# The convolution branch of the gated mixers of a four-layer fp32 model: from behind the attention's projection into the head steps

## The chip, the cores and the metric

One core of a Trainium2 chip runs the whole program in one launch. The metric is the device time of one execution in microseconds (us), lower is better. Everything is fp32; TensorE multiplies in a mode that keeps fewer bits, so each operand is split in a high and a low part.

## What is computed

256 tokens of width 1024 go through two blocks of two layers each. The first block's layer is a gated mixer (heads with a decaying state, and a short convolution) and then a feed-forward network: dense in layer 0, eight experts in layer 1. The second block's layers are of another kind and untouched here. The part that matters, from the reference:

```python
q, f_logit, i_in, g_out, b_gate, c_gate, u, gate_a, gate_b = split_projection(h, w_in)
...
o = hgrn2_chunk_recurrence(qh, k, heads(i_in), log_f)
o = rms_norm(o, g_norm_w) * jax.nn.silu(heads(g_out))
y_a = jnp.einsum('bse,ed->bsd', o.reshape(bsz, seq, HGRN_VAL_WIDTH).astype(h.dtype), w_proj_hgrn)
v = b_gate * u
vp = jnp.pad(v, ((0, 0), (CONV_K - 1, 0), (0, 0)))
conv = conv_w[0] * vp[:, 0:seq, :]
for j in range(1, CONV_K):
    conv = conv + conv_w[j] * vp[:, j:j + seq, :]
y_b = jnp.einsum('bse,ed->bsd', c_gate * conv, w_proj_conv)
merged = jax.nn.sigmoid(gate_a) * y_a + jax.nn.sigmoid(gate_b) * y_b
return jnp.einsum('bsd,de->bse', merged, w_out)
```

## The kernel before, in words

**The stream of weights.** All weights lie in one array of slabs, 128 partitions by 2048 numbers (1 MB), in the order of use. SyncE loads them six ahead into `raw` (`Sync.slabs`). For each, ScalarE copies the high part to `whi` (`hi`, L305, two halves), VectorE subtracts to get the low part in `wlo` (`lo`, L746), and TensorE runs 24 matmuls (`slab`, L1333 to L1335: high by high, low by high, high by low). `whi` holds three slabs: `hi` of slab n waits until slab n-3 is done on TensorE. Each engine runs its instructions in the order written, so the place of a `hi()` or `lo()` among the other calls decides when a slab is ready.

**The mixer** (`mixer1`, for l = 0 and 1). Twelve slabs give the first three of nine column segments. Then four **head steps** (`it` = 0 to 3), two heads each: TensorE turns their inputs (`head_turn`), sums the logs of the decay (`head_sums`), multiplies scores (`head_scores`, L1445) and outputs (`head_out`, L1464). Between these stand six slabs a step (`late_half`): each pair gives 512 columns of a late segment, which `late_group` on ScalarE (L359, L360) copies out. PSUM banks 0 to 3 serve these pairs in turn, banks 4 to 7 the heads. VectorE multiplies the decays (`decay`, L842) and picks the scores (`select`, L855).

**The tail**, twelve slabs, is written out on every engine:
1. ScalarE ends the norm and takes Silu of g_out and Sigmoid of both gates (L447 to L451); VectorE multiplies the heads' output with norm and gate (L891, event `on`) and b_gate with u (L894, `bu`). TensorE waits for `on`, turns the product (L1365) and, once it is split (L317, L763), projects it: a.mm0 and a.mm1, two slabs each.
2. TensorE turns `bu` and c_gate (L1502, four pairs of columns, c0 to c6, 32 transposes) into banks 4 to 7. For each pair VectorE takes the three taps and the product with c_gate straight from PSUM (L910, L914, L917). ScalarE (L460) and VectorE (L921) split the result into XH and XL; then b.mm0 and b.mm1, four slabs.
3. VectorE gates and adds both (L903, L925, L926), TensorE turns the sum (L1365), and w2.mm0, w2.mm1 (four slabs) give the output, which is added to X (L932).

## Time and profile before

| | us |
|---|---|
| median of three runs | 3032.9 (3029.36 to 3033.09) |
| the profiled execution, its own time | 3030.92 |
| its span in the profile | 3029.1 |
| TensorE busy in it | 2849.8 |
| VectorE busy | 2054.6 |
| ScalarE busy | 1686.7 |
| mean granted TensorE clock | 0.973 |

A busy TensorE is not always TensorE at full speed: the granted clock stands beside it in the views by stretch (1.00 is 2.4 GHz, 0.50 is 1.2 GHz). Idle time in brackets is time of that engine just before the instruction, with the instruction that ended it.

### The profile page before, as it was taken

What the parts mean: (1) busy time and instruction counts of PE and PEld (TensorE: products, weight loads), DVE (VectorE), ACT (ScalarE), POOL (GpSimd) and SP (SyncE); (2) the same over time, 40 slices, a digit from 0 to 9 for tenths busy, and PEclk for the clock granted to TensorE, in tenths of its full rate; (3) what the DMA queues carried; (4) which work ended last, traced back from release to release, by engine and by line L of the source; (5) the groups of instructions that cost most, each with busy time, mean ns of one, the idle gap of its engine ahead of it and who ended that gap; (6) DMA issues with size and microseconds to landing.
All of it is one profiled execution on the core that took longest, in us unless ns stands there. A gap on an engine that the chain in (4) does not pass through costs nothing.

```text
span 3029.1 us, 34232 instructions
## 1 busy us (share of the span) xinstructions
PE 2849.8 (94%) x13288; PEld 2355.1 (78%) x13288; DVE 2054.6 (68%) x2910; ACT 1686.7 (56%) x2271; POOL 33.0 (1%) x55
## 2 busy tenths in 40 slices
...
GB/s 230 154 135 111 131 176 185 170 173 139 131 108 163 376 357 347 342 355 357 352 344 352 359 193 183 185 158 148 142 171 184 177 183 192 148 157 147 160 185 107
DMA packets 173657, 633.63 MB, mean 209 GB/s; under 512 B 19520, under 2 KB 19520, under 8 KB 173488
## 3 DMA queue, kind: packets, MB, share of 16 engines
...
## 4 chain that ended last, share of the span: by engine, by line
PE 86%; DVE 9%; ACT 3%; issue 1%; DMA 1%; SPq 0%; DVEq 0%; ACTq 0%; POOLq 0%
PE ps L1333 26%; PE ps L1335 26%; PE ps L1334 26%; DVE wlo L746 2%; PE ps L1445 2%; DVE CA L1207 2%; PE ps L1522 1%; PE ps L1569 1%; PE ps L1365 1%; PE ps L1431 0%; PE ps L1432 0%; DVE XN L914 0%; DVE Z L1294 0%; DMA raw<-in_W 0%; ACT whi L305 0%
## 5 line engine op out<-in xcount | busy, mean ns | idle before, releaser
L746 DVE TENSOR_TENSOR wlo<-raw,whi 128x1024 fp32r<-128x1024 f32 x1182 | 1386.6, 1221 | 539.6 <-ACT whi L305 533.0
L305 ACT ACTIVATE whi<-raw 128x1024 fp32r<-128x1024 f32 x1182 | 1187.7, 1057 | 558.2 <-PE ps L1335 552.3
L1333 PE MATMUL ps<-whi,XH 128*128 128x512 f32 (+1 forms) x2192 | 871.1, 397 | 43.5 <-DVE XL L764 19.8
L1334 PE MATMUL ps<-wlo,XH 128*128 128x512 f32 (+1 forms) x2192 | 857.3, 391 | 0.0
L1335 PE MATMUL ps<-whi,XL 128*128 128x512 f32 (+1 forms) x2192 | 856.6, 391 | 0.0
L1333 PEld LDWEIGHTS ps<-whi,XH 128*128 128x128 f32 x2192 | 416.4, 190 | 137.1 <-DVE XL L764 23.6
L1335 PEld LDWEIGHTS ps<-whi,XL 128*128 128x128 f32 x2192 | 415.8, 190 | 87.9
L1334 PEld LDWEIGHTS ps<-wlo,XH 128*128 128x128 f32 x2192 | 416.5, 190 | 82.4 <-issue 0.5
L1333 PE MATMUL ps<-whi,XEH 128*128 128x512 f32 x704 | 280.8, 399 | 1.4 <-DVE XEL L995 1.4
L1335 PE MATMUL ps<-whi,XEL 128*128 128x512 f32 x704 | 275.3, 391 | 0.0
L1334 PE MATMUL ps<-wlo,XEH 128*128 128x512 f32 x704 | 274.1, 389 | 0.0
L1333 PE MATMUL ps<-whi,GH 128*128 128x512 f32 x440 | 172.2, 391 | 0.0
L1335 PE MATMUL ps<-whi,GL 128*128 128x512 f32 x440 | 171.3, 389 | 0.0
L1334 PE MATMUL ps<-wlo,GH 128*128 128x512 f32 x440 | 171.2, 389 | 0.0
L1335 PEld LDWEIGHTS ps<-whi,XEL 128*128 128x128 f32 x704 | 132.1, 188 | 28.9
L1333 PEld LDWEIGHTS ps<-whi,XEH 128*128 128x128 f32 x704 | 132.2, 188 | 27.7 <-DVE XEL L995 1.6
L1334 PEld LDWEIGHTS ps<-wlo,XEH 128*128 128x128 f32 x704 | 132.5, 188 | 25.9
L484 ACT ACTIVATE GH<-ps 128x512 fp32r<-128x512 f32 x55 | 33.0, 599 | 206.9 <-PE ps L1522 206.9
L952 DVE TENSOR_TENSOR GL<-ps,GH 128x512 fp32r<-128x512 f32 x55 | 38.0, 692 | 162.3 <-ACT GH L484 162.3
L1333 PE MATMUL ps<-whi,GH_ 128*128 128x512 f32 x352 | 144.2, 410 | 0.0
L1335 PE MATMUL ps<-whi,GL_ 128*128 128x512 f32 x352 | 137.4, 390 | 0.0
L1334 PE MATMUL ps<-wlo,GH_ 128*128 128x512 f32 x352 | 137.3, 390 | 0.0
...
## 6 DMA issues: line engine op xcount, KB each, us to landing
...
```

Of the source, the lines that this page charges most:

```text
L305: act.activation(k.whi[:, slot, part], k.raw[:, at, part], ACT.Copy).then_inc(*k.up("act_hi"))
L484: act.activation(GH[:, 2 * g:2 * g + 2, :], src, ACT.Copy).then_inc(*k.up("act_split", f"{T}.gh{g}"))
L746: dve.tensor_tensor(k.wlo[:, at, part], k.raw[:, at, part], k.whi[:, slot, part], ALU.subtract).then_inc(*k.up("dve_lo"))
L952: dve.tensor_tensor(GL[:, 2 * g:2 * g + 2, :], src, GH[:, 2 * g:2 * g + 2, :], ALU.subtract).then_inc(*k.up("dve_split", f"{T}.gl{g}"))
L1207: x = dve.scalar_tensor_tensor(out=CA[:, c, :], in0=HP[:, c, j:j + S], scalar=dw(c, j), in1=CA[:, c, :], op0=ALU.mult, op1=ALU.add)
L1333: pe.matmul(ps, xh, k.whi[:, slot, cols], start=first, stop=False)
L1334: pe.matmul(ps, xh, k.wlo[:, at, cols], start=False, stop=False)
L1335: mm = pe.matmul(ps, xl, k.whi[:, slot, cols], start=False, stop=last)
L1365: mm = pe.transpose(bank[:, i * S + t * P:i * S + (t + 1) * P], src(2 * b + i, t), k.ident[:])
L1445: mm = pe.matmul(o, x, x, start=True, stop=True)
L1522: mm = pe.transpose(turned[:, fb, t * P:(t + 1) * P], GN[:, t, fb * P:(fb + 1) * P], k.ident[:])
L1569: mm = pe.matmul(k.ps[:, 6 + c // 4, (c % 4) * P:(c % 4 + 1) * P], k.XN[:, t, c * P:(c + 1) * P], k.PM[:, t, :], start=t == 0, stop=t == N ...
```

## The change

1. The late segments come in another order (`LATE`, and with it the weights' order in `stream`): the convolution's b, u, c columns first (head steps 0 and 1), then g_out, gate_a, gate_b. The scratch segment `SKN` moves to gate_b's place.
2. In head steps 1 and 2 TensorE turns one pair of columns after `head_sums` and one after the second `head_scores` (`conv_turn`, eight transposes each, 32 in all) into the banks of the late pairs; ScalarE copies them to SBUF (`conv_turned`), into the parts of q and f that are used up.
3. In head steps 1 to 3 VectorE multiplies b by u in two halves (`conv_gate`) and takes the taps, now from SBUF (`conv3`); ScalarE and VectorE split the result into new arrays CVH and CVL (`conv_split`, `conv_rest`). The last half of the last split (`conv_rest(1)`) stands behind the head steps.
4. The tail begins with b.mm0 and the first slab of b.mm1; then TensorE turns the heads' output (now into banks 4 to 7), does the second slab of b.mm1, then a.mm0 and a.mm1. The turning of the merged sum is cut in two (`ya` between the slabs of a.mm1, `yb` after the first slab of w_out), and w_out's slabs come in the order 0, 2, 1, 3. `hi` and `lo`, twelve each as before, are spread singly among this work.

`turned` and `project` get arguments for other targets and for a call between two slabs, nothing else. No instruction is left out; the mixers of both layers change alike. The diff, cut:

```diff
-SKN = SCU
+SKN = SGB
+LATE = [(SCB, 0), (SCU, 0), (SCC, 0), (SCB, 1), (SCU, 1), (SCC, 1), (SGO, 0), (SGO, 1), (SGA, 0), (SGA, 1), (SGB, 0), (SGB, 1)]
+CONV_FREES = {5: 0, 6: 1, 8: 2, 9: 3}
...
+            ("pad3", [P, SCC * SEG], F32), ("CVH", [P, KT, S], F32R), ("CVL", [P, KT, S], F32R),
...
+    def conv_out(self):
+        return self.Z[:, SCU * SEG:(SCU + 1) * SEG].rearrange("p (n c) -> p n c", c=S)
+    def conv_in(self, n):
+        at = (SQ if n % 2 == 0 else SF) * SEG
+        return self.Z[:, at:at + 2 * CW].rearrange("p (i c) -> p i c", i=2)
...
     def late_group(self, T, it, j):
         act, k = self.eng, self.k
-        bank = 2 * ((3 * it + j) % 2)
-        src, at = k.ps[:, bank:bank + NT, :], it * (NT * CW) + (SGA, SGO, SCB)[j] * SEG
-        to = k.Z[:, at:at + NT * CW].rearrange("p (t c) -> p t c", t=NT)
+        n = 3 * it + j
+        bank = 2 * (n % 2)
+        src, to = k.ps[:, bank:bank + NT, :], k.seg(LATE[n][0])[:, LATE[n][1]]
         act.wait_ge(*k.at(f"{T}u{j}.mm.{it}"))
         act.activation(to[:, 0], src[:, 0], ACT.Copy, scale=k.rsin[:, 0:1])
...
+    def conv_turned(self, T, n, bank):
+        act, k = self.eng, self.k
+        act.wait_ge(*k.at(f"{T}c{n}.tp"))
+        if n >= 2:
+            act.wait_ge(*k.at(f"{T}c{n - 2}.y"))
+        act.activation(k.conv_in(n), k.ps[:, bank:bank + 2, :], ACT.Copy).then_inc(*k.up("act_evac", f"{T}c{n}.in"))
+    def conv_split(self, T, g):
+        act, k = self.eng, self.k
+        act.wait_ge(*k.at(f"{T}c{2 * g + 1}.y"))
+        act.activation(k.CVH[:, 4 * g:4 * g + 4, :], k.conv_out()[:, 4 * g:4 * g + 4, :], ACT.Copy).then_inc(*k.up("act_split", f"{T}cv{g}.h"))
...
+            if it == 1 or it == 2:
+                self.conv_turned(T, 2 * it - 2, 2 * (it % 2))
             self.late_group(T, it, 1)
             self.hi()
+            if it >= 2:
+                self.conv_split(T, it - 2)
             self.hi()
+            if it == 1 or it == 2:
+                self.conv_turned(T, 2 * it - 1, 2 * ((it + 1) % 2))
             self.head_cross(T, it)
             self.late_group(T, it, 2)
+            if it == HEADS // 2 - 1:
+                self.hi()
             self.head_out(T, it)
         act.wait_ge(*k.at(f"{T}o1.{HEADS // 2 - 1}"))
         act.activation(k.orn, k.oss, ACT.Sqrt, scale=1.0 / P, bias=k.eps).then_inc(*k.up("act_step", T + "orms"))
-        act.wait_ge(*k.at(f"{T}ev2.{HEADS // 2 - 1}"))
+        act.wait_ge(*k.at(T + "ev1.2"))
         act.activation(k.seg(SGO), k.seg(SGO), ACT.Silu).then_inc(*k.up("act_step", T + "g"))
-        act.activation(k.seg(SGA), k.seg(SGA), ACT.Sigmoid)
-        act.activation(k.seg(SGB), k.seg(SGB), ACT.Sigmoid).then_inc(*k.up("act_step", T + "gates"))
+        self.hi()
+        act.wait_ge(*k.at(T + "ev2.3"))
+        act.activation(k.seg(SGB), k.seg(SGB), ACT.Sigmoid).then_inc(*k.up("act_step", T + "gb"))
+        self.hi()
...
+        self.turned(T + "o", lambda i: gw, bank0=4)
+        self.hi()
+        act.wait_ge(*k.at(T + "ev0.3"))
+        act.activation(k.seg(SGA), k.seg(SGA), ACT.Sigmoid).then_inc(*k.up("act_step", T + "ga"))
+        self.hi(2)
+        self.turned(T + "ya", None, KT // 2, 0, 4, k.CVH)
+        self.hi(2)
+        self.turned(T + "yb", None, KT // 2, KT // 2, 6, k.CVH)
         self.hi(4)
...
+    def conv_gate(self, T, g):
+        dve, k = self.eng, self.k
+        dve.wait_ge(*k.at(f"{T}ev1.{g}"))
+        B = k.seg(SCB)[:, g]
+        dve.tensor_tensor(B, B, k.seg(SCU)[:, g], ALU.mult).then_inc(*k.up("dve_gate", f"{T}bu{g}"))
+    def conv3(self, T, l, n):
+        dve, k = self.eng, self.k
+        CV = k.conv_out()
+        w = lambda j, i: k.pcols[:, l * LCOLS + 17 + 8 * j + i:l * LCOLS + 18 + 8 * j + i]
+        dve.wait_ge(*k.at(f"{T}c{n}.in"))
+        dve.wait_ge(*k.at(f"{T}bu{n // 2}"))
+        pair = [(2 * n + i, k.conv_in(n)[:, i, :]) for i in range(2)]
+        for i, src in pair:
+            c = dve.tensor_scalar(CV[:, i, :], src[:, 0:S], w(2, i), None, ALU.mult)
+        self.step(c)
+        for j in (1, 2):
+            for i, src in pair:
+                c = dve.scalar_tensor_tensor(out=CV[:, i, j:], in0=src[:, 0:S - j], scalar=w(2 - j, i), in1=CV[:, i, j:], op0=ALU.mult, op1=ALU.add)
+            self.step(c)
+        dve.tensor_tensor(CV[:, 2 * n:2 * n + 2, :], CV[:, 2 * n:2 * n + 2, :], k.conv_in(n)[:, :, S:], ALU.mult).then_inc(*k.up("dve_gate", f"{T}c{n}.y"))
+    def conv_rest(self, T, g):
+        dve, k = self.eng, self.k
+        at = slice(4 * g, 4 * g + 4)
+        dve.wait_ge(*k.at(f"{T}cv{g}.h"))
+        dve.tensor_tensor(k.CVL[:, at, :], k.conv_out()[:, at, :], k.CVH[:, at, :], ALU.subtract).then_inc(*k.up("dve_split", f"{T}cv{2 * g + 1}.l"))
...
+            if it == 1 or it == 2:
+                self.conv_gate(T, it - 1)
+            if it >= 2:
+                self.conv3(T, l, 2 * it - 4)
+            if it == 3:
+                self.conv_rest(T, 0)
...
+            if it >= 2:
+                self.conv3(T, l, 2 * it - 3)
...
+        self.lo()
+        self.conv_rest(T, 1)
...
+        self.lo()
+        YA, YB = k.seg(SQ), k.seg(SF)
+        dve.wait_ge(*k.at(T + "gb"))
+        dve.wait_ge(*k.at(T + "b.mm0"))
+        dve.tensor_tensor(YB[:, 0], ps[:, 0:2, :], k.seg(SGB)[:, 0], ALU.mult).then_inc(*k.up("dve_step", T + "b.ev0"))
+        self.lo()
         gw = pc[:, c0 + 16:c0 + 17]
-        self.turned(T + "o", lambda i: gw)
-        YA, YB = k.seg(SQ), k.seg(SF)
+        self.turned(T + "o", lambda i: gw, bank0=4)
+        self.lo()
+        dve.wait_ge(*k.at(T + "b.mm1"))
+        dve.tensor_tensor(YB[:, 1], ps[:, 2:4, :], k.seg(SGB)[:, 1], ALU.mult).then_inc(*k.up("dve_step", T + "b.ev1"))
+        self.lo()
+        dve.wait_ge(*k.at(T + "ga"))
         for j in range(2):
-            self.lo(2)
             dve.wait_ge(*k.at(f"{T}a.mm{j}"))
+            self.step(dve.tensor_tensor(YA[:, j], ps[:, 2 * j:2 * j + 2, :], k.seg(SGA)[:, j], ALU.mult), f"{T}a.ev{j}")
+            dve.tensor_tensor(YA[:, j], YA[:, j], YB[:, j], ALU.add).then_inc(*k.up("dve_gate", f"{T}merged{j}"))
+            self.lo()
             if j == 0:
...
+                self.turned(T + "ya", None, KT // 2, 0, 4, (k.CVH, k.CVL))
+                self.lo()
+        self.turned(T + "yb", None, KT // 2, KT // 2, 6, (k.CVH, k.CVL))
+        self.lo(2)
...
+            self.lo()
             dve.wait_ge(*k.at(f"{T}w2.mm{j}"))
...
+                if n in CONV_FREES:
+                    pe.wait_ge(*k.at(f"{T}c{CONV_FREES[n]}.in"))
...
+    def conv_turn(self, T, n, it, j):
+        pe, k = self.eng, self.k
+        g, bank = n // 2, 2 * ((3 * it + j) % 2)
+        pe.wait_ge(*k.at(f"{T}bu{g}"))
+        pe.wait_ge(*k.at(f"{T}ev2.{g}"))
+        pe.wait_ge(*k.at(f"{T}ev{j}.{it}"))
+        for i in range(2):
+            for a, s in enumerate((SCB, SCC)):
+                for t in range(NT):
+                    c = (2 * n + i) % 4
+                    mm = pe.transpose(k.ps[:, bank + i, a * S + t * P:a * S + (t + 1) * P], k.seg(s)[:, g, t, c * P:(c + 1) * P], k.ident[:])
+        mm.then_inc(*k.up("pe_turn", f"{T}c{n}.tp"))
...
+            if it == 1 or it == 2:
+                self.conv_turn(T, 2 * it - 2, it, 0)
             self.late_half(T, it, 1, 1)
...
+            if it == 1 or it == 2:
+                self.conv_turn(T, 2 * it - 1, it, 1)
             self.late_half(T, it, 2, 1)
...
+        y = lambda half: lambda i, t: YA[:, half, t, i * P:(i + 1) * P]
+        pe.wait_ge(*k.at(T + "ev1.3"))
+        self.project(T + "b.mm0", 0, split=T + "cv", XH=k.CVH, XL=k.CVL)
+        pe.wait_ge(*k.at(T + "ev2.3"))
+        self.project(T + "b.mm1", 2, XH=k.CVH, XL=k.CVL, split=T + "cv", between=lambda: self.turned(
+            T + "o", [T + "on0"], lambda i, t: O[:, i // 4, t, (i % 4) * P:(i % 4 + 1) * P], bank0=4, ready2=[T + "on1"]))
+        pe.wait_ge(*k.at(T + "b.ev0"))
+        self.project(T + "a.mm0", 0, split=T + "o")
+        pe.wait_ge(*k.at(T + "b.ev1"))
+        self.project(T + "a.mm1", 2, split=T + "o", between=lambda: self.turned(T + "ya", [T + "merged0"], y(0), KT // 2, 4))
+        pe.wait_ge(*k.at(T + "ya1.l"))
+        self.slab(self.columns(0, 0, k.CVH, k.CVL))
+        self.turned(T + "yb", [T + "merged1"], y(1), KT // 2, 6)
+        self.slab(self.columns(0, 2, k.CVH, k.CVL))
+        pe.wait_ge(*k.at(T + "yb1.l"))
+        self.slab(self.columns(1, 0, k.CVH, k.CVL), T + "w2.mm0")
+        self.slab(self.columns(1, 2, k.CVH, k.CVL), T + "w2.mm1")
...
+        late = [q[{SGO: 3, SCB: 4, SCC: 5, SCU: 6, SGA: 7, SGB: 8}[s]][l][:, g * CW:(g + 1) * CW] for s, g in LATE]
+        parts.append(column_slabs(np.concatenate([q[n][l] for n in (1, 0, 2)] + late, 1)))
+        parts += [column_slabs(i[n][l]) for n in ("w_proj_conv", "w_proj_hgrn")]
+        parts.append(column_slabs(i["w_out"][l])[[0, 2, 1, 3]])
```

How that moves instructions, at three places. **VectorE, from the last select of head step 2 into head step 3** (L890 was L855, L780 was L746, L853 was L818). Before:

```order
L855 COPY_PREDICATED SM<-masks,ps 128x256 x7
L746 TENSOR_TENSOR wlo<-raw,whi 128x1024 x4
L818 TENSOR_TENSOR LFL<-Z,LFH 128x256 x2
L746 TENSOR_TENSOR wlo<-raw,whi 128x1024 x2
L842 TENSOR_TENSOR XN<-XN,KQ 128x64 x4
```

and changed:

```order
L890 COPY_PREDICATED SM<-masks,ps 128x256 x7
L780 TENSOR_TENSOR wlo<-raw,whi 128x1024 x2
L909 TENSOR_SCALAR Z<-Z,pcols 128x256 x2
L913 SCALAR_TENSOR_TENSOR Z<-Z,pcols 128x255 x2
L913 SCALAR_TENSOR_TENSOR Z<-Z,pcols 128x254 x2
L915 TENSOR_TENSOR Z<-Z 128x512
L922 TENSOR_TENSOR CVL<-Z,CVH 128x1024
L780 TENSOR_TENSOR wlo<-raw,whi 128x1024 x2
L853 TENSOR_TENSOR LFL<-Z,LFH 128x256 x2
L780 TENSOR_TENSOR wlo<-raw,whi 128x1024 x2
```

One pair's taps and half of the low parts now stand ahead of the step's first `lo`; another pair's taps (the same four rows) stand ahead of the decays.

**ScalarE, from the last head's output to the tail's first slabs** (the slab's split, L305, is now L317; L317 before and L329 now split the turned heads' output). Before:

```order
L409 ACTIVATE Z<-ps 128x2x128
L413 ACTIVATE SC,small<-ps 128x128 x2
L447 ACT_TABLE_LOAD
L447 ACTIVATE small<-small 128x16
L449 ACT_TABLE_LOAD
L449 ACTIVATE Z<-Z 128x2048
L450 ACT_TABLE_LOAD
L450 ACTIVATE Z<-Z 128x2048
L451 ACTIVATE Z<-Z 128x2048
L317 ACTIVATE XH<-ps,pcols 128x256
```

and changed:

```order
L421 ACTIVATE Z<-ps 128x2x128
L425 ACTIVATE SC,small<-ps 128x128 x2
L481 ACT_TABLE_LOAD
L481 ACTIVATE small<-small 128x16
L483 ACT_TABLE_LOAD
L483 ACTIVATE Z<-Z 128x2048
L317 ACTIVATE whi<-raw 128x1024 x2
L486 ACT_TABLE_LOAD
L486 ACTIVATE Z<-Z 128x2048
L317 ACTIVATE whi<-raw 128x1024 x2
L329 ACTIVATE XH<-ps,pcols 128x256
```

A slab's high part now stands behind Silu, another behind the one Sigmoid that is left here; a third stands ahead of the last two heads' output (L421, twice).

**VectorE, from the last select to the first gate of the tail.** Before:

```order
L855 COPY_PREDICATED SM<-masks,ps 128x256 x7
L746 TENSOR_TENSOR wlo<-raw,whi 128x1024 x2
L888 RECIPROCAL small<-small 128x16
L891 SCALAR_TENSOR_TENSOR Z<-Z,small 128x128 x16
L894 TENSOR_TENSOR Z<-Z 128x2048
L763 SCALAR_TENSOR_TENSOR XL<-ps,pcols,XH 128x256
```

and changed:

```order
L890 COPY_PREDICATED SM<-masks,ps 128x256 x7
L780 TENSOR_TENSOR wlo<-raw,whi 128x1024 x4
L922 TENSOR_TENSOR CVL<-Z,CVH 128x1024
L965 RECIPROCAL small<-small 128x16
L968 SCALAR_TENSOR_TENSOR Z<-Z,small 128x128 x16
L780 TENSOR_TENSOR wlo<-raw,whi 128x1024 x2
L975 TENSOR_TENSOR Z<-ps,Z 128x1024
L780 TENSOR_TENSOR wlo<-raw,whi 128x1024 x2
L798 SCALAR_TENSOR_TENSOR XL<-ps,pcols,XH 128x256
```

The last low parts of the convolution now wait behind one more `lo`, and the split of the heads' output (L798) behind two `lo` and a gate.

## Rows read from the trace of the kernel before

**Rows 1.** The page's part 4, the chain that ended last, share of the span by engine
```profile
PE 86%; DVE 9%; ACT 3%; issue 1%; DMA 1%; SPq 0%; DVEq 0%; ACTq 0%; POOLq 0%
```

**Rows 2.** Stretches of one core: busy us (instructions) by engine, granted clock, DMA
```profile
228.00:275.00 47.00, 47.00 (x257) 40.55 (x256) 30.56 (x87) 25.30 (x49) 0.00 (x0) 1.00 0.41 135
...
275.90:381.40 105.50, 81.50 (x352) 66.53 (x352) 64.34 (x97) 43.31 (x58) 0.00 (x0) 0.85 0.35 119
...
832.00:937.60 105.60, 81.74 (x353) 66.68 (x352) 64.35 (x97) 43.33 (x58) 2.27 (x5) 0.85 0.38 127
```

**Rows 3.** TensorE by line, 275.9 to 381.4 us: count, busy, mean ns, idle before
```profile
L1333 PE MATMUL ps<-whi,XH 128*128 128x512 f32 x96 | 39.5, 411 | 8.3 <-issue 6.1 <-DVE XL L764 2.1
...
L1502 PE MATMUL ps<-ident,Z 128*128 128x128 f32 x32 | 5.8, 349 | 4.4 <-DVE XN L917 4.4
...
L1365 PE MATMUL ps<-ident,Z 128*128 128x128 f32 x32 | 5.7, 337 | 11.3 <-DVE Z L891 9.5 <-DVE Z L926 1.7
```

**Rows 4.** TensorE in time: start, us, what, count, idle before it and releaser
```profile
275.27 0.61 PE L1464 MATMUL ps<-Z,SC 128*128 128x128 f32 x4
...
285.35 3.73 PE L1365 MATMUL ps<-ident,Z 128*128 128x128 f32 x16 [9.47 <-DVE Z L891]
...
291.22 0.50 PE L1333 MATMUL ps<-whi,XH 128*128 128x512 f32 x1 [2.14 <-DVE XL L764]
...
331.00 0.77 PE L1333 MATMUL ps<-whi,XH 128*128 128x512 f32 x1 [6.06 <-issue]
...
382.69 1.97 PE L1365 MATMUL ps<-ident,X 128*128 128x128 f32 x16 [1.32 <-DVE X L932]
```

**Rows 5.** ScalarE in time, splits of slabs in the tail
```profile
298.60 2.01 ACT L305 ACTIVATE whi<-raw 128x1024 fp32r<-128x1024 f32 x2 [5.76 <-PE ps L1335]
...
304.04 2.01 ACT L305 ACTIVATE whi<-raw 128x1024 fp32r<-128x1024 f32 x2 [3.43 <-PE ps L1335]
...
339.26 2.01 ACT L305 ACTIVATE whi<-raw 128x1024 fp32r<-128x1024 f32 x2 [7.01 <-PE ps L1335]
```

**Rows 6.** TensorE in time, turning the heads' inputs in head step 3
```profile
234.92 0.60 PE L1414 MATMUL ps<-ident,XN 128*128 128x128 f32 x4
...
235.71 0.48 PE L1333 MATMUL ps<-whi,XH 128*128 128x512 f32 x1
```

**Rows 7.** VectorE in time, head step 3 and tail of the first mixer
```profile
234.73 2.36 DVE L746 TENSOR_TENSOR wlo<-raw,whi 128x1024 fp32r<-128x1024 f32 x2 [6.13 <-ACT whi L305]
...
245.42 3.34 DVE L842 TENSOR_TENSOR XN<-XN,KQ 128x64 f32<-128x64 f32 x24 [5.39 <-ACT XN L391]
...
272.49 2.36 DVE L746 TENSOR_TENSOR wlo<-raw,whi 128x1024 fp32r<-128x1024 f32 x2
...
283.11 4.29 DVE L891 SCALAR_TENSOR_TENSOR Z<-Z,small 128x128 f32<-128x128 f32 x16 [3.04 <-ACT Z L449]
...
316.06 0.87 DVE L910 TENSOR_SCALAR XN<-ps,pcols 128x256 f32<-128x256 f32 x2
...
319.45 0.87 DVE L910 TENSOR_SCALAR XN<-ps,pcols 128x256 f32<-128x256 f32 x2
...
381.41 1.23 DVE L932 TENSOR_TENSOR X<-ps,X 128x1024 f32<-128x1024 f32 x1 [1.99 <-PE ps L1335]
```

**Rows 8.** ScalarE in time, head step 3 and what follows it
```profile
241.46 0.69 ACT L359 ACTIVATE Z<-ps,small 128x512 f32<-128x512 f32 x1 [2.92 <-PE ps L1335]
...
265.10 2.00 ACT L305 ACTIVATE whi<-raw 128x1024 fp32r<-128x1024 f32 x2 [5.87 <-PE ps L1335]
...
275.32 0.69 ACT L360 ACTIVATE Z<-ps,small 128x512 f32<-128x512 f32 x1
...
278.18 1.28 ACT L447 ACT_TABLE_LOAD   x1
...
279.48 0.31 ACT L447 ACTIVATE small<-small 128x16 f32<-128x16 f32 x1
...
281.10 1.91 ACT L449 ACTIVATE Z<-Z 128x2048 f32<-128x2048 f32 x1
```

More of the change, by code:

```diff
@@ L306, in hi, with turned @@
             self.n += 1
-    def turned(self, tag, gain, n=KT, at=0, bank0=0):
+    def turned(self, tag, gain, n=KT, at=0, bank0=0, into=None):
         act, k = self.eng, self.k
@@ L752, in step, with turned @@
         self.eng.wait_ge(*self.k.now("dve_step"))
-    def turned(self, tag, gain, n=KT, at=0, bank0=0):
+    def turned(self, tag, gain, n=KT, at=0, bank0=0, into=None):
         dve, k = self.eng, self.k
+        XH, XL = into or (k.XH, k.XL)
         for b in range(n // 2):
@@ L901, in mixer1 @@
             if j == 0:
-                dve.wait_ge(*k.at(T + "gates"))
-            dve.tensor_tensor(YA[:, j], ps[:, 2 * j:2 * j + 2, :], k.seg(SGA)[:, j], ALU.mult).then_inc(*k.up("dve_step", f"{T}a.ev{j}"))
-        CV = flat(k.XN[:]).rearrange("p (n c) -> p n c", c=S)
-        w = lambda j, i: pc[:, c0 + 17 + 8 * j + i:c0 + 18 + 8 * j + i]
-        for n in range(0, KT, 2):
-            pair = [(i, ps[:, 4 + i % 4, :]) for i in (n, n + 1)]
-            dve.wait_ge(*k.at(f"{T}c{n}.tp"))
-            for i, bank in pair:
-                c = dve.tensor_scalar(CV[:, i, :], bank[:, 0:S], w(2, i), None, ALU.mult)
-            self.step(c)
-            for j in (1, 2):
-                for i, bank in pair:
-                    c = dve.scalar_tensor_tensor(out=CV[:, i, j:], in0=bank[:, 0:S - j], scalar=w(2 - j, i), in1=CV[:, i, j:], op0=ALU.mult, op1=ALU.add)
-                self.step(c)
-            for i, bank in pair:
-                c = dve.tensor_tensor(CV[:, i, :], CV[:, i, :], bank[:, S:], ALU.mult)
-            c.then_inc(*k.up("dve_gate", f"{T}c{n}.y"))
@@ L919, in mixer1 @@
-        for i in range(0, KT, 2):
-            dve.wait_ge(*k.at(f"{T}cv{i}"))
-            dve.tensor_tensor(k.XL[:, i:i + 2, :], CV[:, i:i + 2, :], k.XH[:, i:i + 2, :], ALU.subtract).then_inc(*k.up("dve_split", f"{T}cv{i // 2}.l"))
-        for j in range(2):
-            self.lo(2)
-            dve.wait_ge(*k.at(f"{T}b.mm{j}"))
-            self.step(dve.tensor_tensor(YB[:, j], ps[:, 2 * j:2 * j + 2, :], k.seg(SGB)[:, j], ALU.mult), f"{T}b.ev{j}")
-            dve.tensor_tensor(YA[:, j], YA[:, j], YB[:, j], ALU.add).then_inc(*k.up("dve_gate", f"{T}merged{j}"))
```

47 lines of the change are left out of this document (9 added, 38 removed).

## The prediction

> **What bounds the kernel now.** I read the chain of waits first: TensorE carries 86% of the span, VectorE 9% [rows 1]. So only time in which TensorE stands, or runs at the lower clock, can be had without removing work. The view by stretches shows where that is. In a head step TensorE is busy all the time (47.00 of 47.00 us, clock 1.00) while VectorE works 30.6 and ScalarE 25.3. In the two tails it is busy 81.5 of 105.5 and 81.7 of 105.6 us, at a mean clock of 0.85 [rows 2]. TensorE's groups by line name the idle time of the first tail: 8.3 + 4.4 + 11.3 = 24.0 us [rows 3], nearly all in three holes: 9.5 us until the heads' output is normed and gated, 2.1 until it is split, and 6.1 + 4.4 round the convolution's taps [rows 3, 4].
>
> The holes cost a second time, in clock. 16 transposes take 3.73 us behind the first hole and 1.97 at the full clock [rows 4]. Slabs in a row end every 5.44 us (298.60 to 304.04), while the slab begun at 291.22 is done at 298.60 (7.4 us) and the one begun at 331.00 at 339.26 (8.3 us) [rows 4, 5]. That is 1.8 + 1.9 + 2.8 = 6.5 us, and the last 16 of the convolution's transposes, also at half clock, add some 2: 32 of them took 5.8 us of busy time [rows 3]. Together about 8.6 us of clock.
>
> **What the tail needs without holes.** The first tail runs from 275.88 (275.27 + 0.61) to 381.41, when VectorE has the last product: 105.5 us [rows 4, 7]. Its twelve slabs need 12 x 5.44 = 65.3 us, and after the change 16 + 8 + 8 transposes at 1.97 us per 16 = 3.9 us, together 69.2. The convolution's 32 transposes move into the head steps. There eight of them cost 0.79 us from first to next slab (234.92 to 235.71) and some 0.1 of slower restart [rows 6], so 4 x 0.9 = 3.6 us, in a stage where TensorE has no idle time: all of it is paid. Gain per mixer: 105.5 - 69.2 - 3.6 = 32.7 us, which agrees with idle plus clock (24.0 + 8.6 = 32.6). It holds only if each event is early enough. I walk the queues on the clock of the old trace; the 3.6 us shift all engines alike.
>
> **Head steps.** VectorE gets one pair's taps (316.06 to 319.45: 3.4 us) and, at one edge, a half product or half split (1.2 us, as the same size at 381.41) ahead of the step's first `lo`, and 3.4 us ahead of the decays. The waits there are 6.1 and 5.4 us [rows 7], against 4.6 and 3.4: both fit, with 1.5 and 2.0 us left, and 30.6 + 8.0 = 38.6 us of work stays under the step's 47. The trace has the taps only from PSUM. From SBUF I bound them at 2.5 us a pair (three of seven instructions at half price) and 5 (half as long again); at 5 the first wait is overrun by 0.1 and the second not at all. I take 3.4. ScalarE's copy of 1024 columns takes about 1.0 us (two such take 2.00) and it waits 5.9 us in one place of the step [rows 8]; one copy or split at each of three places fits. The evacuation for which the first `conv_turn` of a step waits is made from 241.5 to 242.7, while TensorE has two sums and a whole slab (5.4 us) to do behind the pair's end at 241.2: `conv_turn` can't come before 246.6, so it finds the bank free, 4 us early or more [rows 5, 6, 8]. The second has a slab and the scores before it. If this cover were gone, TensorE would pay the overrun one for one.
>
> **Tail, first event.** Nothing is between the last head and b.mm0's first slab: its weights are ready (`lo` done at 274.85) [rows 7] and half the convolution is split. First slab 275.6 to 281.2. The second needs `conv_rest(1)`, behind a `lo`, behind the new `hi`. ScalarE is free at 275.9 (275.32 + 0.6), `hi` ends at 277.9, `lo` at 279.3, `conv_rest` at 280.5. That is 0.7 us early, the thinnest margin.
>
> **Heads' output.** The new `hi` delays ScalarE by 1.9 us. From table load to Silu's end was 278.18 to 283.0, now to 285.0; the 16 products take 4.3 us [rows 7, 8] and end at 289.4. TensorE has three slabs to run, until 292.1: 2.7 early, so the 9.5 us hole is covered. Its split (0.39 us each, eight, behind two `lo` and one gate) has its first half at 296.9, needed at 299.6.
>
> **Later seams.** Counting 5.44 a slab, 2.0 a `lo` on ScalarE, 2.35 on VectorE, 1.23 a gate or sum: `lo` for the second slab of a.mm1 ends at 315.3 (needed 316.9), the first merged half at 313.0 (315.9), the `lo` of w_out's first slab at 320.8 (322.3), of its second at 327.1 (328.7), of its third at 332.6 (334.2). Each has 1.5 us or more. A stalled `hi` on ScalarE would hold the turned copies behind it; the late one is then `ya`, 4 us ahead of need. The last product ends near 345.2.
>
> The loads move by nothing but their pace: SyncE still waits for the slab six back, and the head stretch moves 135 GB/s, the tail 119 [rows 2]. In the second tail POOL's loads now meet the same slabs. I cost it at 0, at worst 1 us.
>
> **Sum.** Two mixers at 32.7 = 65.4 us; I take off 1.5 for semaphores on thin margins: 64 us. 3030.9 (the profiled execution, 2 below the median of 3032.9) less 64 is **2967 us**. Its own bounds: 2963 (all of it, and a fast draw like the lowest run) to 2973 (3 us lost per mixer).
>
> **A rule against the change.** A table load takes 1.28 us, and the next ScalarE instruction starts 1.30 us after it (278.18 to 279.48) [rows 8]. The Trainium skill, ScalarE: Activation LUTs, section "What ACT_TABLE_LOAD costs", adds a drain of some 1.38 us to each switch of set. By that rule, with Sqrt, Silu and Sigmoid now standing before slabs' splits, the heads' split would be some 4 us later and the sum by its figure about 3 us smaller, 2970. The trace does not show such a drain.
>
> **Rivals.**
> - *The tail keeps small waits* (0.14). For it: 0.7 and 1.5 us are thin, and `lo`, gate and split now alternate in one queue. Against: no length is guessed, all are read. If the second slab and four later seams each come 1.5 to 2.5 us late past need, a mixer loses 4 to 9 us: 2975 to 2985. The table loads are one way to it: if each cost twice its 1.28 us, the two ahead of the products would put the `lo` behind these at 294.3 (needed 294.0), the three ahead of the split would put its first half at 300.7 (needed 299.6): 1.4 us a mixer, 2970.
> - *Head steps 2 and 3 stretch* (0.06). VectorE's longer queue delays `lo` and decays; 2 us in each of four steps give 8 us: 2975. Against: the waits above.
> - *The clock does not come back* (0.05). If the lower clock had another cause than the idle time before it, 2 x 8.6 = 17 us stay: 2984. Against: it falls only behind the holes, and head steps run dense at 1.00 [rows 2].
> - *The change is hidden* (0.02). If the head steps were held as long as the tail gains, within 6 us: 3025 to 3037. I know no cause.
> - *Slower* (0.03). `conv_turn` waits on TensorE for `ev` and `bu`, ahead of a slab; ScalarE's next `hi` waits for that slab, and VectorE's taps for the copy. If this ring closed late in each of the 8 places (4 per mixer), every stall would also bring half clock for a slab (2.8 us). It decides at 65 / 8 = 8.2 us each, a stall of 5.4; at 7 us of stall the kernel takes 2967 + 8 x 9.8 = 3045. Against: `ev` is 4 us early or more, and `bu` needs no more than a gap of VectorE.
>
> The likeliest case has 0.70. The range 2961 to 2979 holds it, with the nearer part of the first two rivals, and leaves out under 2 in 10. Faster by over 0.2% (6 us, about what a measurement can tell here): 0.70 + 0.14 + 0.06 + 0.05 = 0.95; same 0.02; slower 0.03.
>
> **What would show it.** In the changed profile: two tails of 69 to 73 us with clock 0.98 or more; no idle of TensorE over 2 us in them; head steps 1 and 2 longer by 1.8 us each, step 3 not; idle of VectorE in steps 2 and 3 down by 8 and 9 us. The forecast is wrong if TensorE waits for CVL at the tail's second slab by more than 1 us, for XL at a.mm0, or for `lo` at w_out's slabs, or if a wait for the copy of a turned pair shows in a head step.

## The result, and the profile after

The changed kernel takes 2965.8 us (median of four, 2964.75 to 2966.68) against 3033.0 of the kernel before in the same session (3029.36 to 3034.6): 0.978 of its time, 95% interval 0.9763 to 0.9797. The forecast was 2967 in 2961 to 2979. The span fell from 3029.1 to 2962.9 us, by 66.2.

The chain that ended last, share of the span by engine (against [rows 1]):

```profile
PE 88%; DVE 8%; ACT 2%; issue 1%; DMA 1%; SPq 0%; DVEq 0%; ACTq 0%; POOLq 0%
```

By stretch, columns as in [rows 2] (busy us of TensorE, its weight loads, VectorE, ScalarE and GpSimd, then TensorE's granted clock and the DMA's share and rate): head step 2 and head step 3, each from the last output matmuls of one step to those of the next, then the two tails:

```profile
185.57:233.62 48.05, 48.05 (x266) 41.53 (x265) 37.04 (x104) 27.56 (x50) 0.00 (x0) 1.00 0.39 132
233.62:279.89 46.27, 46.27 (x251) 39.82 (x250) 35.83 (x98) 25.62 (x48) 0.00 (x0) 1.00 0.41 137
280.50:349.40 68.90, 68.84 (x320) 57.07 (x319) 47.41 (x62) 40.35 (x54) 0.00 (x0) 1.00 0.54 181
803.00:872.50 69.50, 69.44 (x326) 57.67 (x324) 47.41 (x62) 40.95 (x55) 2.27 (x5) 1.00 0.57 194
```

The tails of [rows 2] had 105.5 us, 81.5 of them busy, at a clock of 0.85. Now TensorE is never without work in them and stays at 1.00. Its groups by line in the first tail (against [rows 3]) have no idle time before any of them; the two other groups from CVH and CVL have 24.9 us each, the three from XH 12.5 us for 32 each. The 32 transposes, heads' output and merged sum, take 4.0 us where they took 5.7:

```profile
L1399 PE MATMUL ps<-whi,CVH 128*128 128x512 f32 x64 | 25.2, 393 | 0.0
...
L1431 PE MATMUL ps<-ident,Z 128*128 128x128 f32 x32 | 4.0, 272 | 0.0
```

TensorE in time, start and length in us, at the tail's two ends (against [rows 4]): the last head, the first slab 0.36 us behind it, the turning of half the merged sum between two slabs, and the only two waits, both behind the mixer:

```profile
279.89 0.61 PE L1549 MATMUL ps<-Z,SC 128*128 128x128 f32 x4
280.25 0.48 PE L1399 MATMUL ps<-whi,CVH 128*128 128x512 f32 x1
...
320.20 1.03 PE L1431 MATMUL ps<-ident,Z 128*128 128x128 f32 x8
320.99 0.48 PE L1399 MATMUL ps<-whi,XH 128*128 128x512 f32 x1
...
350.66 1.97 PE L1431 MATMUL ps<-ident,X 128*128 128x128 f32 x16 [1.32 <-DVE X L998]
353.95 0.50 PE L1399 MATMUL ps<-whi,XH 128*128 128x512 f32 x1 [1.32 <-DVE XL L799]
```

VectorE in time: a pair's taps, the split, the next waits (against [rows 7]), then what the heads' output needs and the two ends of the merged sum:

```profile
232.26 0.61 DVE L909 TENSOR_SCALAR Z<-Z,pcols 128x256 f32<-128x256 f32 x2
232.91 1.79 DVE L913 SCALAR_TENSOR_TENSOR Z<-Z,pcols 128x255 f32<-128x255 f32 x4
234.73 0.69 DVE L915 TENSOR_TENSOR Z<-Z 128x512 f32<-128x512 f32 x1
235.34 1.22 DVE L922 TENSOR_TENSOR CVL<-Z,CVH 128x1024 fp32r<-128x1024 f32 x1
239.34 2.36 DVE L780 TENSOR_TENSOR wlo<-raw,whi 128x1024 fp32r<-128x1024 f32 x2 [2.78 <-ACT whi L317]
...
250.03 3.35 DVE L877 TENSOR_TENSOR XN<-XN,KQ 128x64 f32<-128x64 f32 x24 [2.31 <-ACT XN L403]
...
283.89 1.22 DVE L922 TENSOR_TENSOR CVL<-Z,CVH 128x1024 fp32r<-128x1024 f32 x1
...
289.62 4.29 DVE L968 SCALAR_TENSOR_TENSOR Z<-Z,small 128x128 f32<-128x128 f32 x16 [3.04 <-ACT Z L483]
...
316.28 1.22 DVE L987 TENSOR_TENSOR Z<-Z 128x1024 f32<-128x1024 f32 x1
...
349.38 1.23 DVE L998 TENSOR_TENSOR X<-ps,X 128x1024 f32<-128x1024 f32 x1 [1.95 <-PE ps L1401]
```

ScalarE in time, the table loads (against [rows 8]):

```profile
284.69 1.28 ACT L481 ACT_TABLE_LOAD   x1
285.99 0.31 ACT L481 ACTIVATE small<-small 128x16 f32<-128x16 f32 x1
286.31 1.28 ACT L483 ACT_TABLE_LOAD   x1
287.61 1.92 ACT L483 ACTIVATE Z<-Z 128x2048 f32<-128x2048 f32 x1
```

**The account.** The tail ran from 275.88 to 381.41 (105.5 us) and now from 280.50 to 349.38 (68.9). From the first turning of a head's inputs to the end of the last head it was 95.56 to 275.88 (180.3) and is 96.60 to 280.50 (183.9). So the first mixer loses 36.65 in the tail and pays 3.58 in the head steps: 33.07. The second gains 33.24 (286.02 to 252.78, from its first turning of a head's inputs to the start of its last addition to X), together 66.3. The span has 66.2: the new execution began the head steps 1.04 us later and has 0.9 of this back in the stages behind the second mixer. The loads of GpSimd in the second tail, costed at 0, cost nothing that shows: both intervals are 252.78.

Executions of one kernel differ by 1 to 3 us in stages that the change doesn't touch, so below the runs are also compared by **one interval in the trace: first turning of a head's inputs to start of the last addition to X, first mixer**. It is 285.85 before and 252.78 after.

### The profile page after: what moved, and what is told of

Read it like the earlier page. It is cut to its first block, busy times and chain, and to the rows that moved or that the text cites. A ratio compares the mean times of both kernels' runs of the same rounds, so it can differ in the third digit from the quotient of the medians.

```text
span 2962.9 us, 34242 instructions
## 1 busy us (share of the span) xinstructions
PE 2832.2 (96%) x13288; PEld 2344.1 (79%) x13288; DVE 2052.1 (69%) x2900; ACT 1691.6 (57%) x2275; POOL 33.0 (1%) x55
## 4 chain that ended last, share of the span: by engine, by line
PE 88%; DVE 8%; ACT 2%; issue 1%; DMA 1%; SPq 0%; DVEq 0%; ACTq 0%; POOLq 0%
PE ps L1399 26%; PE ps L1401 26%; PE ps L1400 26%; DVE wlo L780 2%; PE ps L1530 2%; DVE CA L1273 2%; PE ps L1610 1%; PE ps L1657 1%; PE ps L1431 1%; PE ps L1516 1%; PE ps L1517 1%; DVE Z L1360 0%; DMA raw<-in_W 0%; ACT whi L317 0%; DVE X L1210 0%
## 5 line engine op out<-in xcount | busy, mean ns | idle before, releaser
L780 DVE TENSOR_TENSOR wlo<-raw,whi 128x1024 fp32r<-128x1024 f32 x1182 | 1386.6, 1222 | 487.9 <-ACT whi L317 481.5
L317 ACT ACTIVATE whi<-raw 128x1024 fp32r<-128x1024 f32 x1182 | 1186.7, 1057 | 492.3 <-PE ps L1401 489.4
L1399 PE MATMUL ps<-whi,XH 128*128 128x512 f32 (+1 forms) x2064 | 818.6, 397 | 28.6 <-DVE XL L799 16.2
L1401 PE MATMUL ps<-whi,XL 128*128 128x512 f32 (+1 forms) x2064 | 805.0, 390 | 0.0
L1400 PE MATMUL ps<-wlo,XH 128*128 128x512 f32 (+1 forms) x2064 | 804.9, 390 | 0.0
L1399 PEld LDWEIGHTS ps<-whi,XH 128*128 128x128 f32 x2064 | 391.2, 190 | 114.5 <-DVE XL L799 19.1
L1401 PEld LDWEIGHTS ps<-whi,XL 128*128 128x128 f32 x2064 | 390.9, 189 | 82.2
L1400 PEld LDWEIGHTS ps<-wlo,XH 128*128 128x128 f32 x2064 | 391.6, 190 | 76.6 <-issue 0.5
L1401 PE MATMUL ps<-whi,XEL 128*128 128x512 f32 x704 | 275.9, 392 | 0.0
```

What stands on the lines that cost most here:

```text
L317: act.activation(k.whi[:, slot, part], k.raw[:, at, part], ACT.Copy).then_inc(*k.up("act_hi"))
L780: dve.tensor_tensor(k.wlo[:, at, part], k.raw[:, at, part], k.whi[:, slot, part], ALU.subtract).then_inc(*k.up("dve_lo"))
L1399: pe.matmul(ps, xh, k.whi[:, slot, cols], start=first, stop=False)
L1400: pe.matmul(ps, xh, k.wlo[:, at, cols], start=False, stop=False)
L1401: mm = pe.matmul(ps, xl, k.whi[:, slot, cols], start=False, stop=last)
```

## The experiments

Each run stands against the kernel before on its own chip. c_after is the changed kernel once more. "Interval" is the one just named. Lines of the diffs are against the changed kernel, of e1 against the kernel before.

| run | median us | ratio to before (95%) | interval |
|---|---|---|---|
| c_after | 2965.55 | 0.9778 (0.9764 to 0.9792) | 252.78 |
| e1_filler | 3023.80 | 0.9972 (0.996 to 0.9984) | 281.84 |
| e2_attention_first | 2996.93 | 0.9878 (0.9863 to 0.9893) | 267.37 |
| e3_hi_late | 2969.60 | 0.9791 (0.9778 to 0.9805) | 254.40 |
| e4_whole_turn | 2972.10 | 0.9800 (0.9786 to 0.9813) | 255.07 |
| e5_taps_twice | 2962.88 | 0.9769 (0.9754 to 0.9784) | 252.77 |
| e6_taps_four | 2993.92 | 0.9869 (0.9854 to 0.9884) | 268.64 |
| e7_turn_twice | 2972.45 | 0.9802 (0.9787 to 0.9817) | 256.28 |
| e8_half_seam | 2964.52 | 0.9774 (0.9761 to 0.9787) | 252.79 |
| e9_seam_clear | 2962.91 | 0.9768 (0.9756 to 0.9781) | 252.77 |
| e10_taps_three | 2968.11 | 0.9786 (0.9772 to 0.9800) | 255.57 |
| e11_attention_first_filler | 2997.98 | 0.9888 (0.9873 to 0.9902) | 267.58 |

### What the lower clock was worth: e1_filler

The kernel before, with transposes that nobody reads put into the tail's holes.

```diff
+        self.filler(4, 72)
         self.turned(T + "o", [T + "on0"], ...
+        self.filler(4, 28)
...
+                pe.wait_ge(*k.at(T + "a.ev0"))
+                self.filler(0, {4: 22, 6: 17}[n])
                 pe.wait_ge(*k.at(f"{T}c{n - 4}.y"))
...
+            if j == 0:
+                self.filler(0, 54)
```

> The kernel before, with turnings of the identity whose result nobody reads put on TensorE into its waits of both tails (72 before the heads' product is turned, 28 behind it, 22 and 17 in the taps, 54 before b.mm0; 0.123 us each by the 16 in 1.97 us). All other work and every wait stay. It separates the clock from the idle time. My theory (the lower clock follows the holes, and only the two slabs behind holes are slow on the path, 1.9 and 2.8 us each; the slow transposes are hidden behind VectorE, which sets the holes' ends): 4.7 us per mixer, 3033 - 9 = 3024. Rival, the whole clock share of 8.6 us per mixer is on the path: 3016. Rival, the lower clock has another cause than TensorE standing: 3033, with both slabs still at 7.4 and 8.3 us.

The tail by stretch, then TensorE in time round the first hole:

```profile
276.80:378.30 101.50, 95.09 (x546) 81.69 (x544) 64.36 (x97) 43.39 (x58) 0.00 (x0) 1.00 0.37 123
```

```profile
276.68 8.02 PE L1372 MATMUL ps<-ident 128*128 128x128 f32 x72
286.31 1.09 PE L1365 MATMUL ps<-ident,Z 128*128 128x128 f32 x8 [1.61 <-DVE Z L891]
288.41 1.09 PE L1365 MATMUL ps<-ident,Z 128*128 128x128 f32 x8 [1.01 <-DVE Z L891]
289.34 3.22 PE L1372 MATMUL ps<-ident 128*128 128x128 f32 x28
```

With the holes filled the clock is 1.00 and the interval 4.01 us shorter (4.09 in the second mixer). The first slab takes 5.7 us, from its first matmul at 292.32 to ScalarE's split at 298.06 that waits for its end, where it took 7.4; the convolution's first takes 5.8 (8.3) [rows 5]. So the lower clock came with TensorE's idle time and goes when that is filled, and of the 8.6 us of clock that the prediction found some 4.0 lay on the path. The rest lay beside VectorE: the eight transposes take 1.09 us and then wait 1.01 for the second half of the products.

### What covers the heads' output: e2_attention_first

Taps and transposes stay in the head steps, but the attention's projection comes first again, with its gate, splits and weights in that order.

```diff
+        self.turned(T + "o", [T + "on0"], ... ready2=[T + "on1"])
         pe.wait_ge(*k.at(T + "ev1.3"))
+        self.project(T + "a.mm0", 0, split=T + "o")
+        pe.wait_ge(*k.at(T + "ev2.3"))
+        self.project(T + "a.mm1", 2, split=T + "o")
+        pe.wait_ge(*k.at(T + "a.ev0"))
         self.project(T + "b.mm0", 0, split=T + "cv", XH=k.CVH, XL=k.CVL)
```

> The changed kernel with the attention's projection first again: the taps stay in the head steps, but the tail turns the heads' product at once, projects a.mm0, a.mm1, then b.mm0, b.mm1 (both Sigmoids ahead of the split, the single hi and lo behind it). It separates moving the taps from moving the projection. My theory: the first hole is back (9.5 us, and 0.5 until the split, as VectorE no longer multiplies b by u there) with its clock (1.8 + 1.9): 13.7 us per mixer, 2966 + 27 = 2993. Rival, the taps were nearly all of it: under 2975. Rival, the order is all of it, and taps in the tail cost little: above 3015.

TensorE in time, the turning and the first matmul of the slab; then by stretch the whole slab in the first mixer and the same slab in the second:

```profile
290.60 4.07 PE L1425 MATMUL ps<-ident,Z 128*128 128x128 f32 x16 [9.46 <-DVE Z L961]
295.80 0.77 PE L1393 MATMUL ps<-whi,XH 128*128 128x512 f32 x1 [1.13 <-issue]
```

```profile
295.80:303.00 7.20, 7.20 (x25) 5.86 (x26) 4.87 (x7) 2.29 (x5) 0.00 (x0) 0.79 0.01 2
835.76:841.48 5.72, 5.72 (x25) 4.77 (x26) 4.87 (x7) 2.29 (x4) 0.00 (x0) 1.00 0.02 4
```

The hole of [rows 4] is back to a hundredth (9.46 against 9.47), in both mixers, and the lower clock with it. The interval is 14.59 us longer than after the change: 9.46 + 1.13 idle, about 2 for slow transposes and 1.8 for the slow slab. Against the kernel before it is 18.48 shorter.

The second mixer has the same hole and the same slow transposes (4.08 us), but there the clock was back at 1.00 when the slab began. The slab took 5.7 us instead of 7.2, and the interval is 265.90: 13.12 longer than after the change, 20.12 shorter than before. So the gain of 33 us divides into 18.5 to 20 for the convolution's work in the head steps and 13 to 14.6 for its projection coming first, when the steps are made in this order. The work in the head steps alone gives 56 to 61% of it. The projection alone, with the taps still in the tail, was not run; what that would give is not shown.

### The margins: e3_hi_late and e4_whole_turn

e3 puts the split that was moved ahead of the last `head_out` behind it. e4 turns the merged sum in one piece and takes w_out's slabs in the order 0 to 3.

```diff
+            self.head_out(T, it)
             if it == HEADS // 2 - 1:
                 self.hi()
-            self.head_out(T, it)
```

> The changed kernel with the one hi that stands ahead of the last heads' output moved behind it (two mixers). It tries the margin that I called the thinnest, 0.7 us. My theory: ScalarE's split of that slab ends 2.3 us later, conv_rest(1) with it, so TensorE waits 1.6 us at the second slab of b.mm0: +1.6 per mixer, 2969, with the wait put down to CVL. Rival, there was more room than I read: 2966 and no wait.

```diff
-        self.project(T + "a.mm1", 2, split=T + "o", between=lambda: self.turned(T + "ya", ...
...
+        self.project(T + "a.mm1", 2, split=T + "o")
+        self.turned(T + "y", [T + "merged0"], ... ready2=[T + "merged1"])
+        for j in range(2):
+            self.project(f"{T}w2.mm{j}", 2 * j, split=T + "y", XH=k.CVH, XL=k.CVL)
```

> The changed kernel with the merged sum turned in one piece behind a.mm1, and w_out's slabs in the usual order (0, 1, 2, 3), as before the change. My theory: the wait of 1.7 us for the second merged half is back, and with the first slab's split some 1.9 us per mixer in all: 2970. Rival, it costs nothing since two slabs follow anyway: 2966. Rival, it also brings half clock for a slab (2.8 us): 2975.

TensorE in time, the wait that each brings, in e3:

```profile
287.34 0.50 PE L1399 MATMUL ps<-whi,CVH 128*128 128x512 f32 x1 [1.35 <-DVE CVL L922]
```

and in e4:

```profile
328.20 1.09 PE L1427 MATMUL ps<-ident,Z 128*128 128x128 f32 x8 [1.70 <-DVE Z L985]
```

e3's interval is 1.62 us longer. The moved `hi` takes 2.0 us; 0.7 of that was margin, and the rest shows, 1.35 of it as this wait. The thinnest margin of the prediction is thereby measured from the other side. In e4 the second half of the sum is waited for (1.70) and the interval is 2.29 longer. Both waits come again in the second mixer (1.36, 1.71). By twice the interval's difference e4 should take 2970.2; its median stands 1.9 us above, its profiled execution, the lowest of five, 2.3 below.

### What the work in the head steps costs: e5, e10, e6 and e7

e5, e10 and e6 take each pair's taps two, three and four times into the same place; e7 turns each pair twice. The output doesn't change.

```diff
-        for i, src in pair:
-            c = dve.tensor_scalar(CV[:, i, :], src[:, 0:S], w(2, i), None, ALU.mult)
...
+        for _ in range(2):
             for i, src in pair:
...
+                c = dve.tensor_scalar(CV[:, i, :], src[:, 0:S], w(2, i), None, ALU.mult)
             self.step(c)
+            for j in (1, 2):
...
```

> The changed kernel with each pair's three taps computed twice on VectorE in head steps 2 and 3 (the same numbers again, +2.4 us at four places per mixer). My theory: VectorE still waits 2.8 us ahead of the first lo and 2.3 ahead of the decays in the changed profile, so both are just filled and TensorE loses nothing or under 0.5 us a step: 2966 to 2968. Rival, the head steps were already at VectorE's edge: +2.4 at each of 8 places, 2985.

> The same with the taps computed four times (+7.2 us at each place). My theory: VectorE's work in steps 2 and 3 is 36.3 + 14.4 = 50.7 us against TensorE's 46.3, so VectorE becomes the bound of four steps: at least 4.4 us each, up to 7 where it still has to wait for exps and scores: 2984 to 2994, with waits of TensorE for the decays' products. Rival, taps in head steps are hidden whatever their length: 2966.

> The taps computed three times (+4.8 us at each of four places per mixer), between e5 (no loss) and e6 (8 us a step). By plain work VectorE has 36.3 + 9.6 = 45.9 us of a step of 46.3, and the step would still be TensorE's: 2966 to 2968. My theory after e6: a wait of 3.2 us for the first scores' product stands inside the step whatever VectorE's queue holds, so its room ends near 43 us: 2 to 4 us in each of four steps, 2974 to 2982.

VectorE with the taps twice, the same place in head step 3 as above:

```profile
237.00 1.22 DVE L923 TENSOR_TENSOR CVL<-Z,CVH 128x1024 fp32r<-128x1024 f32 x1
238.50 2.36 DVE L780 TENSOR_TENSOR wlo<-raw,whi 128x1024 fp32r<-128x1024 f32 x2 [0.28 <-ACT whi L317]
...
249.28 3.34 DVE L877 TENSOR_TENSOR XN<-XN,KQ 128x64 f32<-128x64 f32 x24
```

TensorE with the taps three times, its only waits in head steps 2 and 3:

```profile
223.24 3.36 PE L1531 MATMUL ps<-E 128*128 128x128 f32 x28 [0.71 <-DVE SM L890]
...
272.21 3.36 PE L1531 MATMUL ps<-E 128*128 128x128 f32 x28 [1.60 <-DVE SM L890]
```

and four times, in head step 2, with the stretch of the last row beside it:

```profile
215.71 3.39 PE L1531 MATMUL ps<-XN 128*128 128x128 f32 x28 [1.05 <-DVE XN L864]
...
228.09 4.99 PE L1531 MATMUL ps<-E 128*128 128x128 f32 x28 [3.07 <-DVE SM L890]
```

```profile
228.09:233.08 4.99, 4.99 (x30) 4.99 (x31) 2.25 (x2) 0.00 (x0) 0.00 (x0) 0.66 0.27 110
```

Another 2.4 us for every pair costs nothing: the wait of 2.78 us shrinks to 0.28, the one ahead of the decays is gone, and the interval stands (252.77). Its median even lies 2.7 us under c_after's, on another chip. The second mixer ends at the same time in both (its last addition to X starts at 872.0), so the difference is made in the untouched stages behind it, and is no gain of the added taps. With 4.8 us more a pair the interval grows by 2.8, with 7.2 by 15.9. My own forecast for e10 (2974 to 2982) was wrong: I had taken the step from two to four as a ramp. The first overrun meets waits of VectorE further down the same step (1.60 us for the scores at 227.08 in e10) and is mostly absorbed; past that the price is more than the added work: the step from three to four adds 9.6 us of taps in four places and 13.1 us to the interval. In each of the two steps TensorE then waits three times (1.02, 1.05 and 3.07 us in step 2), and the scores behind the longest wait run at a granted clock of 0.66, 4.99 us instead of 3.39. So the head steps had room for 2.4 to 4.8 us more a pair than the change puts there.

```diff
-        for i in range(2):
+        for i in (0, 1, 0, 1):
```

> The changed kernel with each conv_turn's eight transposes made twice (32 more per mixer, same banks, same waits). My theory: TensorE has no idle time in head steps, so each set is paid in full, 0.9 us in 8 places: 2966 + 7 = 2973. Rival, they fall into slack: 2966.

16 transposes instead of 8 in each of four places make the interval 3.50 us longer: 0.88 a set, where the prediction had 0.9 from [rows 6]. No wait appears, so the ring of waits that the slower rival needed doesn't close even with twice the work in it.

### The seam behind the mixer: e8_half_seam and e9_seam_clear

What is left at the end of the tail is the wait for the last addition to X and for the split behind it, 4.57 us from 349.38 to 353.95. e8 lets the next norm's turning begin on X's first half. e9 also takes small VectorE work (tables of the router, rows of the biases) from between the addition and the split to ahead of the addition. The diff is that of e9; e8 has its lines on `out` and `out0` alone.

```diff
+            if j:
+                self.bias_rows() if l else self.router_tables()
             dve.wait_ge(*k.at(f"{T}w2.mm{j}"))
...
-            dve.tensor_tensor(xs, ps[:, 2 * j:2 * j + 2, :], xs, ALU.add).then_inc(*k.up("dve_x", T + "out"))
+            dve.tensor_tensor(xs, ps[:, 2 * j:2 * j + 2, :], xs, ALU.add).then_inc(*k.up("dve_x", T + ("out" if j else "out0")))
...
-        self.router_tables()
...
-        self.bias_rows()
...
-        self.norm_in("f0n", ["m0.out"])
+        self.norm_in("f0n", ["m0.out0"], ["m0.out"])
...
-        self.norm_in("e.n", ["m1.out"])
+        self.norm_in("e.n", ["m1.out0"], ["m1.out"])
```

> The changed kernel, and the seam behind each mixer opened as inside its tail: the feed-forward's (or router's) turning of X waits for the first half of the output only, and for the second half in its middle. My theory: the 1.3 us wait before the turning goes and the split of the first half starts earlier, 1.7 us per mixer: 2962.5. Rival, the split of X, not its turning, ends the seam, and it waits for the second half anyway: under 1 us in all, 2966.

> e8, and the small VectorE work that stood between the last sum of each mixer and the split of X (0.75 us behind the first mixer, 0.4 behind the second) moved ahead of that sum, where VectorE waits 1.95 us. e8 gained 1.0 us at the first seam where I wrote 1.7, and the profile shows this work in front of the split. My theory: it hid the rest, so another 0.7 and 0.4 us; against the changed kernel about 3.5 us in all: 2962.5. Rival, ScalarE's part of the split is what ends the seam: no difference from e8.

> The changed kernel itself, beside the next three, so that all are read against a run of their own. 2966.

TensorE in time at the seam, e8:

```profile
348.60 1.03 PE L1431 MATMUL ps<-ident,X 128*128 128x128 f32 x8
350.08 1.09 PE L1431 MATMUL ps<-ident,X 128*128 128x128 f32 x8 [0.45 <-DVE X L998]
352.35 0.50 PE L1399 MATMUL ps<-whi,XH 128*128 128x512 f32 x1 [1.18 <-DVE XL L799]
```

and e9:

```profile
350.30 1.09 PE L1431 MATMUL ps<-ident,X 128*128 128x128 f32 x8 [0.45 <-DVE X L1000]
352.04 0.50 PE L1399 MATMUL ps<-whi,XH 128*128 128x512 f32 x1 [0.65 <-DVE XL L799]
```

From last addition to first slab: 4.57 us, 3.55 in e8 (348.80 to 352.35), 3.02 in e9 (349.02 to 352.04). At the second mixer, up to the turning of the router's logits, it is 7.27, 5.88 and 5.73. Together that is 2.4 us in e8, where I had forecast 1.7 a mixer, and 3.1 in e9. What e9 adds to e8 is 0.5 us at the first seam and 0.15 at the second, where 0.7 and 0.4 were forecast. e8's median stands 1.0 us under c_after's, on another chip, which the medians alone can't tell from scatter. On the same chip c_after took 2965.43 to 2966.59 and e9 2960.27 to 2963.67 in five executions, 3.3 us less by the medians (2965.55 and 2962.28), which agrees with the 3.1. A sixth execution of e9 took 10166 us; it stands in the median of the table (2962.91) but not in the ratio, and its cause is unknown.

### Does the clock alone explain e2's slow slab? e11_attention_first_filler

e2 with 80 unread transposes in its hole.

```diff
+        self.filler(4, 80)
         self.turned(T + "o", ...
```

> e2 (attention's projection first) with 80 unread turnings of the identity on TensorE in its 9.5 us wait. My theory: the wait stays, the 16 transposes behind it fall from 4.1 to 2.0 us (here the split follows them at once, so that counts) and the slab from 7.2 to 5.4: 3.7 us per mixer, 2997 - 7 = 2990. Rival, the clock share counts for nothing in this order: 2997.

TensorE in time and then by stretch, the last one being the same slab in the second mixer:

```profile
279.47 8.90 PE L1432 MATMUL ps<-ident 128*128 128x128 f32 x80
289.11 1.09 PE L1425 MATMUL ps<-ident,Z 128*128 128x128 f32 x8 [0.74 <-DVE Z L961]
291.21 1.09 PE L1425 MATMUL ps<-ident,Z 128*128 128x128 f32 x8 [1.01 <-DVE Z L961]
294.30 0.47 PE L1393 MATMUL ps<-whi,XH 128*128 128x512 f32 x1 [2.00 <-issue]
```

```profile
288.40:294.30 5.90, 2.18 (x16) 1.74 (x17) 4.51 (x16) 5.90 (x10) 0.00 (x0) 1.00 0.00 0
294.30:296.00 1.70, 1.70 (x7) 1.44 (x8) 1.70 (x5) 1.70 (x4) 0.00 (x0) 0.93 0.00 0
296.00:298.00 2.00, 2.00 (x6) 1.52 (x6) 2.00 (x3) 0.59 (x1) 0.00 (x0) 0.50 0.00 0
...
832.68:841.16 8.48, 8.48 (x25) 6.80 (x26) 4.87 (x7) 2.28 (x4) 0.00 (x0) 0.66 0.00 0
```

Here my forecast of 2990 failed: the interval of the first mixer is that of e2 (267.58 against 267.37). The transposes run at full clock, but VectorE's products set their end, so nothing is won. The slab begins at full clock and falls to half in its middle, behind a stretch of 5.9 us in which TensorE worked 2.18; it takes 7.4 us. In the second mixer, behind the same work, it begins at half clock and takes 8.5; the interval there is 268.69 against 265.90 in e2, whose slab had the full clock. So filling the hole did not decide the slab's clock, and over both mixers it won nothing. In e1, 28 more transposes stood behind the two groups of eight, up to the slab, and the slab ran at 1.00 in both mixers. That makes the thin stretch the likely cause here, but e11 with that stretch filled too was not run.

## Why the prediction was right

The forecast was 1.2 us above the median; 64 us were predicted, 66.2 measured in the profiled executions. That it came so near is in part luck: it started from the profiled execution, 2.1 us under the median of the kernel before, and by the medians the gain is 67.2 us. The two errors, 2.1 too low in the start and 3.2 too little in the gain, largely cancel. By its own steps:

- **Tail, 105.5 to 69.2**: measured 68.9 in both mixers, 0.1 us under the 69 to 73 given as the sign. The slabs' pace of 5.44 and the transposes at full clock held.
- **Price in the head steps, 3.6**: measured 3.58. The steps took 46.26 us each and take 48.04, 48.05 and 46.27: steps 1 and 2 longer by 1.8, step 3 not. e7 gives 0.88 a set.
- **No waits**: the 1.5 us taken off for thin margins were not needed. That is the larger part of the 2 us missed.
- **The walk on the old clock**: all of the new trace is 4.62 us later at the last head (1.04 of it start, 3.58 the transposes). With that added, `conv_rest(1)` was forecast to end at 285.1 and ends at 285.11, the heads' products at 294.0 and 293.91, the merged half at 317.6 and 317.50. Others are less near: the first half of the heads' split ends at 301.2 (301.5), the tail at 349.38 (349.8). The margin of 0.7 us is real: 285.11 against the second slab at 285.79, and e3 uses it up.
- **VectorE in the head steps**: a pair's taps take 3.1 us (0.61 + 1.79 + 0.69), not 3.4: the first tap costs 0.61 for two from SBUF where it cost 0.87 from PSUM [rows 7]; the other two taps cost the same from both (1.79 and 1.78 for four). The Trainium skill, VectorE: DVE Perf Modes, section "Why PSUM operands drop a tier", has fp32 reads of PSUM at the single rate; the rows of the first tap agree. The waits left are 2.78 and 2.31 us where 1.5 and 2.0 were forecast. One of the signs given was wrong: idle of VectorE was to fall by 8 and 9 us in steps 2 and 3, and fell by 5.3 (16.3 to 48.05 - 37.04 = 11.0) and 5.9 (16.3 to 46.27 - 35.83 = 10.4; the old trace has 29.98 and 29.96 us of work in steps of 46.26). I had put the added work down whole, with 3.4 a pair, part of which stands in the neighbouring step, and forgotten that a step that grows by 1.8 us gives VectorE that time too.
- **The split of the check, 24.0 idle + 8.6 clock**: right as time of TensorE, wrong as causes apart. Only 4.0 of the clock was on the path (e1). As both went together, the sum didn't suffer.
- **The rule on table loads**: the load at 284.69 takes 1.28 us and the next instruction starts 1.30 after the load's start, twice in a row. The Trainium skill, ScalarE: Activation LUTs, section "What ACT_TABLE_LOAD costs", has a drain of 1.38 on top. These rows don't show it, and the products end where the walk without it put them.

The other outcomes that the prediction named did not come: small waits in the tail (no wait there at all; e4 shows what one costs), stretched head steps (needs over 2.4 us more a pair), a clock that stays low (e1 and the new trace rule it out), the ring (e7). What stays open is the scatter of stages that the change doesn't touch: the granted clock from 19 to 41 us is 0.88 in one execution of the changed kernel and 1.00 in another, and no run says why.
